# Expert weights in runs of 16 KB: packing the matrices so that one descriptor carries a partition's whole share

## The chip, the cores and the metric

The kernel runs on one core of one Trainium2 chip. The metric is device time in microseconds (us), the median of three runs of the kernel before: 660.63 us (658.98 to 662.78). The profile is of one more execution. Five engines matter: TensorE (PE, with its weight loads, PEld), VectorE (DVE), ScalarE (ACT), GpSimd (POOL) and SyncE (SP). SP, ACT and POOL also issue the transfers; all transfers of the core are carried out by the same 16 DMA engines. In the profile the queue of SP is q1, that of ACT q10 and that of POOL q0.

## What is computed

One layer of a hybrid decoder for 512 prompt tokens and 8 sample tokens, all float32: a mixer (an input projection, a gated recurrence on 512 channels and one on another 512, an output projection), then a hierarchical mixture of experts, then a final norm. Only the last part carries this change's weight:

```python
xn = rmsnorm(x, ln2_g)                       # 520 tokens x 1024
group = argmax(xn @ wg + bg)                 # 1 of 4 groups
top2  = two best of 8 experts in that group  # logits xn @ we[group] + be[group]
for each of 32 experts e, for its tokens:
    h = silu(xn @ w1[e]) * (xn @ w3[e])      # w1, w3: 1024 x 256
    y += gate * (h @ w2[e])                  # w2: 256 x 1024
out = rmsnorm(x + y, final_g)
```

Each of w1, w3 and w2 of an expert is 1 MB, so the 32 experts read 96 MB of weights from device memory, and every expert's weights are read whole, whatever the number of its tokens.

## The kernel before, in words

The mixer takes the first 310 us of the profile. Its input and output projections go by chunks of 2 MB (`w_in` in six chunks of 512 columns, `w_out` in two), which SP loads into the two halves of tile WC (L424).

Then the tokens are routed, and the experts are worked off in 16 pairs of two experts each (two experts side by side in TensorE's columns, up to 64 tokens each). Even pairs (called A below) use weight slots 0 and 1, odd pairs (B) slots 2 and 3. Slot 0 is in the tile SLOT0, slot 1 in SLOT1, slots 2 and 3 in WC and GY (w1 and w3) and in WC (w2). Expert 29 has a place of its own (XNT, XS).

For each pair n there are five pieces of work:

- the gather (POOL, L597): an indirect DMA that brings the 128 token rows of the pair (4 KB each) from `xn_rows` into T. A row without a token is skipped by its index, but leaves a 4-byte packet;
- the turn (PE, L1617): eight transposes of those rows, then DVE scales them into XRC;
- up (PE, L1629): 16 products with w1 and w3 of the two experts, each recorded as two instructions; ACT and DVE make h of it;
- down (PE, L1653): the products with w2; ACT (L824) and DVE (L1299) copy the result out;
- the scatter (POOL, L609): an indirect DMA that writes the rows to `expert_rows`.

TensorE's order is written out by hand: turn(n+1), up(n), down(n-1), transpose of h(n), then the same with n one higher. POOL's order is: gather(n+3), scatter(n), gather(n+4), scatter(n+1), and so on: gather(n+4) stands behind scatter(n), which waits for the copies behind down(n).

The weight loads wait for their slot: SP loads w1 and w3 of a slot (L439) when up with that slot has ended (semaphore h_written); ACT loads w2 (L392) when down has ended, before it copies the result. Four experts and expert 29 are loaded ahead, 27 in the loop. Each load is 128 partitions wide. For w1 and w3 the eight k of a partition lie one after the other in device memory, 8 KB, but in the slot the columns of w1 and w3 alternate by k:

```python
W13 = [s[:, 0:4096].rearrange("p (k f) -> p k f", k=KD) for s in (SLOT0, SLOT1, WCF, GYF)]      # L231
sp.dma_start(w13[:, :, half * FE:(half + 1) * FE],                                              # L439
             w[0, e].rearrange("(p k) f -> p k f", k=KD)).then_inc(s_w13[slot], 16)
```

so that a run without a break is 256 numbers, 1 KB, and a 1 MB load is 1024 packets. A w2 load has runs of 8 KB (128 packets), a chunk of `w_in` or `w_out` runs of 2 KB.

Of the kernel before, what the change touches and what calls it, by code (L numbers as in the profile page):

```python
# [25 lines left out]
P = 128  # L26
# [4 lines left out]
KD = D // P  # L31
# [6 lines left out]
NE = GROUPS * PER_GROUP  # L38
FE = 256
CAP = 64  # L40
# [3 lines left out]
KEPT = NE - 3  # L44
# [14 lines left out]
ORDER = [XR, FX, Q, V, GR, G]  # L59
# [35 lines left out]

def build(nc, x_prompt, x_sample, state_hgrn, state_rglru, state_conv, lower_bounds, ln1_g, w_in,
          hgrn_norm_g, conv_w, conv_b, lru_wx, lru_bx, lru_wa, lru_ba, lru_lambda, w_out, ln2_g,
          router_wg, router_bg, router_we, router_be, exp_w1, exp_w3, exp_w2, final_g,
          y_prompt, y_sample, hgrn_p, rglru_p, conv_p, hgrn_s, rglru_s, conv_s):

    xn_dram = nc.dram_tensor("xn_rows", (TOK, D), F32).ap()
# [9 lines left out]
    with ExitStack() as ctx:  # L111
# [10 lines left out]
        WC = sb("WC", [P, 2, KD, 512])  # L122
        SLOT0 = sb("SLOT0", [P, 6144])
# [5 lines left out]
        SLOT1 = sb("SLOT1", [P, 3 * NH * TOK])  # L129
# [94 lines left out]
        XGT = [XRC[:, 1024 * j:1024 * (j + 1)].rearrange("p (k t) -> p k t", k=KD) for j in range(2)]  # L224
# [3 lines left out]

        GYF = GY[:, :, :].rearrange("p m t -> p (m t)")
        WCF = WC[:, :, :, :].rearrange("p a k t -> p (a k t)")  # L230
        W13 = [s[:, 0:4096].rearrange("p (k f) -> p k f", k=KD) for s in (SLOT0, SLOT1, WCF, GYF)]  # L231
        W2 = [s.rearrange("p (j d) -> p j d", j=2)
              for s in (SLOT0[:, 4096:6144], SLOT1[:, 4096:6144], WCF[:, 4096:6144], WCF[:, 6144:8192])]

        XNF = XNT[:, :, :].rearrange("p k t -> p (k t)")
# [2 lines left out]
        OUT = [SLOT1[:, D * c:D * (c + 1)] for c in range(NT)]  # L238


        W13_KEPT = XNF[:, 0:4096].rearrange("p (k f) -> p k f", k=KD)
        W2_KEPT = XS[:, :, :]
        FGB = T[:, 0, 4:6, :].rearrange("p a t -> p (a t)")

# [1 line left out]
        PS = [ctx.enter_context(nc.psum_tensor(f"ps{b}", [P, 512], F32)) for b in range(8)]  # L246
# [5 lines left out]
        s_wc = [sem(f"wc_in{i}") for i in range(2)]  # L252
# [83 lines left out]
        s_w13 = [sem(f"w13_in{i}") for i in range(5)]  # L336
# [52 lines left out]
            return VEC[:, v + m:v + m + 1]  # L389

        def load_w2(eng, e, slot):
            eng.dma_start(W2[slot], exp_w2[0, e].rearrange("(p j) d -> p j d", j=2)).then_inc(s_w2[slot], 16)  # L392

        def weights_of(p, two, kept):

# [4 lines left out]
        def loads(slot, r, n):  # L400

            if slot == 4:
                return 1
            return r * (NPAIR // 2 - (slot == KEPT % 4)) + n
# [4 lines left out]
        @block.sync  # L409
        def _(sp):  # L410
            sp.dma_start(X[:, 0, :], x_rows(0)).then_inc(s_x[0], 16)
            for i in range(1, NT):
                sp.dma_start(X[0:ROWS[i], i, :], x_rows(i)).then_inc(s_x[i], 16)
            w_in_v = w_in[0].rearrange("(p k) n -> p k n", k=KD)
            w_out_v = w_out[0].rearrange("(m p) n -> p m n", p=P)
            sp.dma_start(G1[:], ln1_g[0].rearrange("(p k) -> p k", k=KD)).then_inc(s_gain[0], 16)

            rows = [(lower_bounds, LB, 8), (hgrn_norm_g, HGG, 4), (conv_w[0], CW, 16), (conv_b, CB, 4), (lru_bx, BX, 4),
                    (lru_ba, BA, 4), (lru_lambda, LAM, 4), (state_rglru[0], H0, NS * NH)]
            for j in range(8):  # L420
                if j >= 2:
                    sp.wait_ge(s_wc_free, j - 1)
                src = w_in_v[:, :, ORDER[j] * 512:(ORDER[j] + 1) * 512] if j < 6 else w_out_v[:, :, (j - 6) * 512:(j - 5) * 512]
                sp.dma_start(WC[:, j % 2, :, :], src).then_inc(s_wc[j % 2], 16)  # L424
                if j == 0:
                    for src, at, n in rows:
                        sp.dma_start(PROW[at:at + n, :], src.rearrange("a (m p) -> (a m) p", p=P)).then_inc(s_par, 16)
                    sp.dma_start(CROW[:], state_conv[0].rearrange("b w (m p) -> (b w m) p", p=P)).then_inc(s_par, 16)
                if j == 1:
                    sp.dma_start(G2[:], ln2_g[0].rearrange("(p k) -> p k", k=KD)).then_inc(s_gain[1], 16)  # L430
                    sp.dma_start(WGt[:], router_wg[0].rearrange("(p k) g -> p (k g)", k=KD)).then_inc(s_rt, 16)
                    sp.dma_start(WEt[:], router_we[0].rearrange("g (p k) e -> p g (k e)", k=KD)).then_inc(s_rt, 16)
                    sp.dma_start(RB[:, 0:GROUPS], router_bg[0:1, :].to_broadcast([P, GROUPS])).then_inc(s_rt, 16)
                    sp.dma_start(RB[:, GROUPS:], router_be.rearrange("a g e -> a (g e)").to_broadcast([P, NE])).then_inc(s_rt, 16)

            def load_w13(e, slot, w13=None):
                w13 = W13[slot] if w13 is None else w13
                for half, w in enumerate((exp_w1, exp_w3)):
                    sp.dma_start(w13[:, :, half * FE:(half + 1) * FE],  # L439
                                 w[0, e].rearrange("(p k) f -> p k f", k=KD)).then_inc(s_w13[slot], 16)  # L440


            sp.wait_ge(s_y, NH + 1)
            sp.wait_ge(s_hp, 16 * NH)
            for e in range(2):
                load_w13(e, e)
                load_w2(sp, e, e)


            for i, c in enumerate(TILE_ORDER):  # L450
                sp.wait_ge(s_xs, NT + i + 1)
                sp.dma_start(xn_dram[c * P:c * P + ROWS[c], :], XS[0:ROWS[c], i % 2, :]).then_inc(s_xn[i % 2], 16)
            sp.dma_start(FGB, final_g.rearrange("(a d) -> a d", a=1).partition_broadcast(P)).then_inc(s_fg, 16)

            sp.wait_ge(s_opr, 2 * NT)
            for e in range(2, 4):
                load_w13(e, e)
                load_w2(sp, e, e)
            await_read(sp, ("lg", NT - 1))
            for i in range(2):  # L460
                sp.wait_ge(s_xg[i], 16)
            load_w13(KEPT, 4, W13_KEPT)
            for i in range(2):
                sp.wait_ge(s_xn[i], 16 * ((NT + 1 - i) // 2))
            sp.dma_start(W2_KEPT, exp_w2[0, KEPT].rearrange("(p j) d -> p j d", j=2)).then_inc(s_w2[4], 16)

            sp.wait_ge(s_rnd, 1)
            rounds = sp.value_load(NRND[0:1, 0:1], min_val=1, max_val=MAX_ROUNDS)
            with sp.Fori(0, rounds) as r:
                with sp.If(r > 0):  # L470

                    sp.wait_ge(s_yw, r * NE)
                    for e in range(4):
                        load_w13(e, e)
                        load_w2(sp, e, e)
                with sp.Fori(0, NE // 4 - 2) as i:
                    for slot in range(4):
                        sp.wait_ge(s_hw, r * NE + i * 4 + slot + 1)
                        load_w13(i * 4 + slot + 4, slot)
                for slot in range(4):  # L480
                    if NE - 4 + slot != KEPT:
                        sp.wait_ge(s_hw, r * NE + NE - 8 + slot + 1)
                        load_w13(NE - 4 + slot, slot)


            sp.wait_ge(s_rdone, rounds + 1)
            ye_v = ye_dram.rearrange("(t k) d -> t k d", k=2)
            for c in range(NT):
                sp.dma_start(YE[c][0:ROWS[c]], ye_v[c * P:c * P + ROWS[c]]).then_inc(s_ye[c], 16)
            for c in range(NT):  # L490
                sp.wait_ge(s_fin[c], 1)
                sp.dma_start(y_rows(c), OUT[c][0:ROWS[c]]).then_inc(s_out, 16)
            sp.wait_ge(s_out, 16 * NT)
# [870 lines left out]
        def _(pe):  # L1364
# [255 lines left out]
            def up(n, p, r, use, kept=False):  # L1620

                pe.wait_ge(s_xgt, 2 * n + 3)
                weights = [weights_of(p, two, kept) for two in range(2)]
                for w13, _, slot in weights:
                    pe.wait_ge(s_w13[slot], 32 * loads(slot, r, use + 1))
                for k in range(KD):
                    for two in range(2):
                        at = two * CAP
                        ins = pe.matmul(PS[2 + p][at:at + CAP, :], XGT[p][:, k, at:at + CAP], weights[two][0][:, k, :],  # L1629
                                        start=(k == 0), stop=(k == KD - 1), tile_position=(0, at), skip_group_check=True)  # L1630
                        if k == KD - 1:
                            ins.then_inc(s_hw, 1)
# [69 lines left out]

_INS = ["x_prompt", "x_sample", "state_hgrn", "state_rglru", "state_conv", "lower_bounds", "ln1_g", "w_in",
        "hgrn_norm_g", "conv_w", "conv_b", "lru_wx", "lru_bx", "lru_wa", "lru_ba", "lru_lambda", "w_out", "ln2_g",
        "router_wg", "router_bg", "router_we", "router_be", "exp_w1", "exp_w3", "exp_w2", "final_g"]
_OUTS = [(1, SEQ, D), (NS, 1, D), (1, 1, NH, P, P), (1, 1, 512), (1, 1, 3, 512),
         (1, NS, NH, P, P), (1, NS, 512), (1, NS, 3, 512)]

# [17 lines left out]
```

## Time and profile before

| | |
|---|---|
| time, median of 3 runs (lowest, highest) | 660.63 us (658.98, 662.78) |
| profiled execution, first to last instruction | 656.5 us |
| PE busy | 510.5 us (78%), mean granted clock 0.88 |
| DVE, ACT, POOL busy | 230.2, 142.6, 79.2 us |
| bytes moved | 144.62 MB, 90494 packets, of which 72197 under 2 KB |
| q1 (SP) | 79608 packets, 100.57 MB |
| q10 (ACT) | 3888 packets, 28.31 MB |
| q0 (POOL) | 6976 packets, 15.44 MB |

The profile is read by stages. From 0 to 310 us TensorE is busy nearly throughout and the DMA engines a third of the time. From 310 to 351 us the tokens are routed and the first pairs start. From 351 to 605 us the DMA engines are busy throughout and TensorE stops and starts. From 605 us on the last pair is finished, the expert rows are read back, combined and written. A granted clock of 1.00 is 2.4 GHz, 0.50 is 1.2 GHz.

### The profile page before, as it was taken

To read this page: it belongs to the slowest core of one execution; us is meant where nothing else is said; L and a number is where in the kernel's file an instruction comes from. 1 tells how busy PE (TensorE), PEld (TensorE's weight loads), DVE (VectorE), ACT (ScalarE), POOL (GpSimd) and SP (SyncE) were. 2 spreads that over 40 slices of the span, in tenths; PEclk is the share of its full clock that TensorE was granted. 3 is DMA by queue.
4 is the path that set the end of the run, shared out by engine and by line. 5 is a ranking of instruction groups with operands and counts; after the bars stand their busy time and mean duration, and the time that the engine had idled before them with its cause. 6 is when DMAs were issued, how large, how long until landed. Compare 5 with 4: busy or idle time off the path is not lost. (4 is left out here: it accounts for less than half of the span.)

```text
span 656.5 us, 6560 instructions
## 1 busy us (share of the span) xinstructions
PE 510.5 (78%) x2320; PEld 296.6 (45%) x2320; DVE 230.2 (35%) x519; ACT 142.6 (22%) x267; POOL 79.2 (12%) x129
## 2 busy tenths in 40 slices
PE   3999999999999989999459839395684929478800
PEld 3788888358888733545333313132231313123200
DVE  3353112694987565233721111111020111101158
ACT  7211044704256352212100000000010000001123
POOL 4000000100211211000030111102011111101014
PEclk9899999999999979999559869788795969779955
DMA  9403110412341439210969999999999999969263
GB/s 300 151 0 129 57 72 12 152 53 77 100 165 64 144 122 308 116 44 22 342 230 331 375 376 337 388 336 394 336 369 376 355 379 331 398 198 381 82 280 130
DMA packets 90494, 144.62 MB, mean 220 GB/s; under 512 B 6489, under 2 KB 72197, under 8 KB 85856
## 3 DMA queue, kind: packets, MB, share of 16 engines
q1 hardware_dynamic: 79608, 100.57, 45.9%
q10 hardware_dynamic: 3888, 28.31, 10.6%
q0 software_dynamic: 6976, 15.44, 7.1%
q8 instruction: 14, 0.23, 0.2%
q14 instruction: 8, 0.07, 0.0%
HBM read 137.49 MB, written 15.10 MB: 232 GB/s over the span
## 5 line engine op out<-in xcount | busy, mean ns | idle before, releaser
L1390 PE MATMUL ps<-XNT,WC 128*128 128x260 f32 x640 | 144.8, 386 | 1.2 <-PE ps L1390 0.6
L1390 PEld LDWEIGHTS ps<-XNT,WC 128*128 128x128 f32 x640 | 121.9, 192 | 23.3 <-issue 4.0
L1629 PE MATMUL ps<-WC,XRC 128*64 128x512 f32 x128 | 69.0, 700 | 66.7 <-DMA GY<-in_exp_w 66.7
L1294 DVE TENSOR_TENSOR XRC<-ps,XRC 128x256 f32<-128x256 f32 x16 | 6.8, 424 | 184.2 <-ACT XRC L810 184.2
L1629 PE MATMUL ps<-GY,XRC 128*64 128x512 f32 x128 | 69.0, 701 | 0.0
L1629 PEld LDWEIGHTS ps<-WC,XRC 128*64 128x64 f32 x128 | 19.8, 162 | 107.7 <-issue 107.6
L1629 PE MATMUL ps<-SLOT,XRC 128*64 128x512 f32 x240 | 59.0, 617 | 2.4 <-DMA SLOT<-in_exp_w 2.4
L1551 PE MATMUL ps<-WC,GY 128*128 128x512 f32 x128 | 58.6, 611 | 1.0 <-DVE GY L1184 0.6
L810 ACT ACTIVATE XRC<-ps 128x256 f32<-128x256 f32 x16 | 6.1, 383 | 209.2 <-PE ps L1629 209.2
L609 POOL DMA_INDIRECT expert_rows<-T,SIDX x16 | 16.1, 1008 | 236.9 <-ACT T L824 220.1
L1551 PEld LDWEIGHTS ps<-WC,GY 128*128 128x128 f32 x128 | 24.4, 196 | 29.4 <-issue 28.2
L1629 PEld LDWEIGHTS ps<-SLOT,XRC 128*64 128x64 f32 x240 | 18.1, 142 | 37.4 <-issue 34.1
L1617 PE MATMUL ps<-IDENT,T 128*128 128x128 f32 x128 | 19.3, 299 | 14.0 <-DMA T<-xn_rows,GIDX 12.7
L1289 DVE TENSOR_TENSOR XRC<-ps,G 128x512 f32<-128x512 f32 x32 | 20.6, 685 | 25.8 <-PE ps L1617 25.8
L1653 PE MATMUL ps<-WC,XRC 128*64 128x512 f32 x128 | 28.9, 593 | 0.6 <-ACT XRC L814 0.6
L1653 PE MATMUL ps<-SLOT,XRC 128*64 128x512 f32 x120 | 28.9, 592 | 0.0
L1439 PE MATMUL ps<-WC,XNT 128*128 128x512 f32 x64 | 28.2, 596 | 0.3 <-DVE Vt L1022 0.3
L1299 DVE COPY T<-ps 128x512 f32<-128x512 f32 x16 | 11.1, 691 | 44.3 <-PE ps L1653 44.3
L1617 PEld LDWEIGHTS ps<-IDENT,T 128*128 128x128 f32 x128 | 16.8, 197 | 15.6 <-issue 13.7
L824 ACT ACTIVATE T<-ps 128x512 f32<-128x512 f32 x16 | 9.6, 597 | 64.7 <-issue 50.3
L1374 PE MATMUL ps<-IDENT,XS 128*128 128x128 f32 (+1 forms) x80 | 13.6, 320 | 10.4 <-ACT XS L669 10.3
L1629 PEld LDWEIGHTS ps<-GY,XRC 128*64 128x64 f32 x128 | 19.9, 163 | 0.0
(273 smaller groups left out, 587.7 us busy)
## 6 DMA issues: line engine op xcount, KB each, us to landing
SLOT<-in_exp_w SPq DMA_DIRECT2D x32, 1024.0 KB, 12.4
WC<-in_exp_w SPq DMA_DIRECT2D x18, 1024.0 KB, 13.3
GY<-in_exp_w SPq DMA_DIRECT2D x16, 1024.0 KB, 17.7
WC<-in_exp_w ACTq DMA_DIRECT2D x14, 1024.0 KB, 8.5
SLOT<-in_exp_w ACTq DMA_DIRECT2D x13, 1024.0 KB, 8.8
WC<-in_w_in SPq DMA_DIRECT2D x6, 2048.0 KB, 9.2
WC<-in_w_out SPq DMA_DIRECT2D x2, 2048.0 KB, 7.8
X<-in_x_prompt SPq DMA_DIRECT2D x4, 512.0 KB, 4.7
```

The source lines that it names most:

```text
L609: pool.indirect_dma_start(out=ye_dram, out_offset=bass.IndirectOffsetOnAxis(ap=SIDX[:, p, :].bitcast(U32), axis=0), in_=YO[p], in_offset=None,
L824: act.activation(YO[p][:, 0:512], PS[5][:, :], ACT.Copy).then_inc(s_ya, 1)
L1289: dve.tensor_tensor(XGT[p][:, 4 * j:4 * j + 4, :], PS[j][:, :].rearrange("p (k t) -> p k t", k=4), bc(G2[:, 4 * j:4 * j + 4], 2, P), ALU.m ...
L1294: dve.tensor_tensor(HG[p], PS[2 + p][:, FE:2 * FE], HS[p], ALU.mult).then_inc(s_hg, 1)
L1299: dve.tensor_copy(YO[p][:, 512:1024], PS[6][:, :]).then_inc(s_yd, 1)
L1374: ins = pe.transpose(ps[:, k * P:k * P + n], xv[:, 4 * j + k, :], IDENT[0:n, 0:n])
L1390: ins = pe.matmul(ps[:, 0:HALF], WC[:, j % 2, k, m * P:(m + 1) * P], XNT[:, k, hf * HALF:(hf + 1) * HALF], start=(k == 0), stop=(k == KD - 1))
L1439: ins = pe.matmul(ps[:, :], XNT[:, k, c * P:(c + 1) * P], WC[:, 1, k, :], start=(k == 0), stop=(k == KD - 1))
L1551: ins = pe.matmul(ps[:, :], rows, weights, start=(j == 0), stop=(j == 2 * NH - 1), skip_group_check=True)
L1617: ins = pe.transpose(PS[k // 4][:, (k % 4) * P:(k % 4 + 1) * P], xv[:, k, :], IDENT[:])
L1629: ins = pe.matmul(PS[2 + p][at:at + CAP, :], XGT[p][:, k, at:at + CAP], weights[two][0][:, k, :], start=(k == 0), stop=(k == KD - 1), tile ...
L1653: ins = pe.matmul(PS[5 + half][at:at + CAP, :], HT[p][:, j, at:at + CAP], weights[two][1][:, j, half * 512:(half + 1) * 512], start=(j == ...
```

## The change

Three arrays become one. `kernel()` lays w1, w3 and w2 of an expert side by side, by partition: `exp_w[e, p]` has 2048 numbers of w1, 2048 of w3 and 2048 of w2. The slot takes the same order (w1 whole, then w3 whole), so that one transfer of 16 KB runs brings what two transfers of 1 KB runs brought; the semaphore of a slot counts 16 for it and no longer 32. The w2 run stays 8 KB, with 24 KB instead of 8 KB between the starts of two runs in device memory. The up product reads its 512 moving columns as two pieces of 256. `w_in` and `w_out` are laid out chunk by chunk, with 16 KB runs. The same bytes are moved to the same tiles.

```diff
-        W13 = [s[:, 0:4096].rearrange("p (k f) -> p k f", k=KD) for s in (SLOT0, SLOT1, WCF, GYF)]
+        W13 = [s[:, 0:4096].rearrange("p (two k f) -> p two k f", two=2, k=KD) for s in (SLOT0, SLOT1, WCF, GYF)]
...
         def load_w2(eng, e, slot):
-            eng.dma_start(W2[slot], exp_w2[0, e].rearrange("(p j) d -> p j d", j=2)).then_inc(s_w2[slot], 16)
+            eng.dma_start(W2[slot], exp_w[e, :, 4096:].rearrange("p (j d) -> p j d", j=2)).then_inc(s_w2[slot], 16)
...
-                src = w_in_v[:, :, ORDER[j] * 512:(ORDER[j] + 1) * 512] if j < 6 else w_out_v[:, :, (j - 6) * 512:(j - 5) * 512]
-                sp.dma_start(WC[:, j % 2, :, :], src).then_inc(s_wc[j % 2], 16)
+                src = w_in[ORDER[j]] if j < 6 else w_out[j - 6]
+                sp.dma_start(WC[:, j % 2, :, :].rearrange("p k n -> p (k n)"), src).then_inc(s_wc[j % 2], 16)
...
             def load_w13(e, slot, w13=None):
                 w13 = W13[slot] if w13 is None else w13
-                for half, w in enumerate((exp_w1, exp_w3)):
-                    sp.dma_start(w13[:, :, half * FE:(half + 1) * FE],
-                                 w[0, e].rearrange("(p k) f -> p k f", k=KD)).then_inc(s_w13[slot], 16)
+                sp.dma_start(w13.rearrange("p two k f -> p (two k f)"), exp_w[e, :, 0:4096]).then_inc(s_w13[slot], 16)
...
                 for w13, _, slot in weights:
-                    pe.wait_ge(s_w13[slot], 32 * loads(slot, r, use + 1))
+                    pe.wait_ge(s_w13[slot], 16 * loads(slot, r, use + 1))
...
-                        ins = pe.matmul(PS[2 + p][at:at + CAP, :], XGT[p][:, k, at:at + CAP], weights[two][0][:, k, :],
+                        out = PS[2 + p][at:at + CAP, :].rearrange("t (two f) -> t two f", two=2)
+                        ins = pe.matmul(out, XGT[p][:, k, at:at + CAP], weights[two][0][:, :, k, :],
                                         start=(k == 0), stop=(k == KD - 1), tile_position=(0, at), skip_group_check=True)
...
+    inputs["exp_w"] = _np.concatenate([inputs.pop(name)[0].reshape(NE, P, -1) for name in ("exp_w1", "exp_w3", "exp_w2")], axis=2)
+    inputs["w_in"] = inputs["w_in"][0].reshape(P, KD, 6, 512).transpose(2, 0, 1, 3).reshape(6, P, KD * 512)
+    inputs["w_out"] = inputs["w_out"][0].reshape(KD, P, 2, 512).transpose(2, 1, 0, 3).reshape(2, P, KD * 512)
```

The order on PE, DVE, ACT and POOL stays as it was. On SP, in the loop over the experts, the load of a slot is two transfers behind one wait in the kernel before (SLOT0, SLOT1, WC and GY are slots 0 to 3; `in_exp_w1` and `in_exp_w3` are w1 and w3):

```order
L439 ISA [waits h_written]
L439 DMA SLOT0<-in_exp_w1 128x8x256
L439 DMA SLOT0<-in_exp_w3 128x8x256
L478 REGISTER_ALU
L439 ISA [waits h_written]
L439 DMA SLOT1<-in_exp_w1 128x8x256
L439 DMA SLOT1<-in_exp_w3 128x8x256
```

In the kernel after, the same place on SP reads:

```order
L436 ISA [waits h_written]
L436 DMA SLOT0<-in_exp_w 128x4096
L474 REGISTER_ALU
L436 ISA [waits h_written]
L436 DMA SLOT1<-in_exp_w 128x4096
```

Two transfers of 128x8x256 have become one of 128x4096 behind the same wait; nothing else has moved.

## Rows read from the trace of the kernel before

**Rows 1.** Stretches of the loop: bounds, length, engines' busy us (count), granted clock, DMA share, GB/s.

```profile
351.40:390.40 39.00, 25.37 (x117) 9.53 (x117) 6.09 (x10) 2.51 (x6) 4.93 (x8) 0.87 1.06 370
390.40:578.60 188.20, 128.84 (x580) 50.13 (x581) 24.04 (x40) 12.55 (x30) 24.49 (x40) 0.82 1.05 363
```

**Rows 2.** Waits of PE from 280 to 620 us: total, times, longest.

```profile
PE ps L1629 <- DMA GY<-in_exp_w: 66.7, 7, 11.5
PE ps L1617 <- DMA T<-xn_rows,GIDX: 12.7, 6, 6.1
```

**Rows 3.** Weight loads of w1 and w3 as SP issues them: start, us.

```profile
399.25 1.25 SPq L439 DMA_DIRECT2D WC<-in_exp_w  x2
...
411.15 18.88 SPq L439 DMA_DIRECT2D SLOT<-in_exp_w  x4
...
587.07 1.25 SPq L439 DMA_DIRECT2D WC<-in_exp_w  x2
```

**Rows 4.** Timeline of one cycle of two pairs: start, us, engine, line, what.

```profile
390.40 1.08 PE L1629 MATMUL ps<-WC,XRC 128*64 128x512 f32 x1 [11.25 <-DMA GY<-in_exp_w]
...
398.90 3.62 PE L1653 MATMUL ps<-SLOT,XRC 128*64 128x512 f32 x16
...
403.78 7.09 PE L1629 MATMUL ps<-SLOT,XRC 128*64 128x512 f32 x32
...
405.24 1.02 POOL L609 DMA_INDIRECT expert_rows<-T,SIDX  x1 [21.54 <-ACT T L824]
...
407.31 1.04 POOL L597 DMA_INDIRECT T<-xn_rows,GIDX  x1 [0.85 <-POOL GIDX L594]
...
414.51 0.86 ACTq L392 DMA_DIRECT2D WC<-in_exp_w  x2
...
415.55 1.16 PE L1617 MATMUL ps<-IDENT,T 128*128 128x128 f32 x8 [0.82 <-DMA T<-xn_rows,GIDX]
...
426.91 1.08 PE L1629 MATMUL ps<-WC,XRC 128*64 128x512 f32 x1 [10.21 <-DMA GY<-in_exp_w]
```

**Rows 5.** Transfers by queue, 430 to 434 us: packets, MB, share.

```profile
q1 hardware_dynamic: 1375, 1.39, 109.6%
```

**Rows 6.** Transfers, 630.5 to 638.5 us: the reading of expert rows.

```profile
DMA packets 462, 3.38 MB, mean 422 GB/s; under 512 B 50, under 2 KB 50, under 8 KB 50
```

**Rows 7.** Transfers by queue, 411.5 to 412.5 us.

```profile
q10 hardware_dynamic: 45, 0.37, 88.8%
q1 hardware_dynamic: 46, 0.05, 12.9%
q0 software_dynamic: 47, 0.00, 2.7%
```

**Rows 8.** Transfers by queue, 405.3 to 409.4 us, all queues that moved.

```profile
q1 hardware_dynamic: 730, 0.74, 56.4%
q10 hardware_dynamic: 106, 0.87, 52.5%
```

**Rows 9.** Transfers of q0, 409.4 to 414.9 us.

```profile
q0 software_dynamic: 288, 0.45, 21.8%
```

**Rows 10.** Page, queues of the whole execution, packets, MB, share: the instruction queue.

```profile
q8 instruction: 14, 0.23, 0.2%
```

**Rows 11.** PE in the first pair, 335 to 350 us.

```profile
335.92 1.97 PE L1617 MATMUL ps<-IDENT,T 128*128 128x128 f32 x8 [6.13 <-DMA T<-xn_rows,GIDX]
...
341.17 7.71 PE L1629 MATMUL ps<-SLOT,XRC 128*64 128x512 f32 x32
```

**Rows 12.** The last cycle: PE at the start of pair 15.

```profile
605.35 1.08 PE L1629 MATMUL ps<-WC,XRC 128*64 128x512 f32 x1 [2.64 <-DMA GY<-in_exp_w]
```

**Rows 13.** Waits of PE from 0 to 260 us: the longest but one.

```profile
PE ps L1504 <- DVE XS L1108: 2.0, 1, 2.0
```

**Rows 14.** Transfers by queue, 339.1 to 343.6 us, all queues that moved.

```profile
q1 hardware_dynamic: 1196, 1.21, 86.5%
```

**Rows 15.** POOL from 339 us: the third gather.

```profile
339.09 1.03 POOL L597 DMA_INDIRECT T<-xn_rows,GIDX  x1 [0.85 <-POOL GIDX L594]
```

More of the change, by code:

```diff
@@ L97, in build @@
           hgrn_norm_g, conv_w, conv_b, lru_wx, lru_bx, lru_wa, lru_ba, lru_lambda, w_out, ln2_g,
-          router_wg, router_bg, router_we, router_be, exp_w1, exp_w3, exp_w2, final_g,
+          router_wg, router_bg, router_we, router_be, exp_w, final_g,
           y_prompt, y_sample, hgrn_p, rglru_p, conv_p, hgrn_s, rglru_s, conv_s):
@@ L238, in build @@
         OUT = [SLOT1[:, D * c:D * (c + 1)] for c in range(NT)]
-        W13_KEPT = XNF[:, 0:4096].rearrange("p (k f) -> p k f", k=KD)
+        W13_KEPT = XNF[:, 0:4096].rearrange("p (two k f) -> p two k f", two=2, k=KD)
         W2_KEPT = XS[:, :, :]
@@ L413, in _ @@
                 sp.dma_start(X[0:ROWS[i], i, :], x_rows(i)).then_inc(s_x[i], 16)
-            w_in_v = w_in[0].rearrange("(p k) n -> p k n", k=KD)
-            w_out_v = w_out[0].rearrange("(m p) n -> p m n", p=P)
             sp.dma_start(G1[:], ln1_g[0].rearrange("(p k) -> p k", k=KD)).then_inc(s_gain[0], 16)
@@ L464, in _ @@
                 sp.wait_ge(s_xn[i], 16 * ((NT + 1 - i) // 2))
-            sp.dma_start(W2_KEPT, exp_w2[0, KEPT].rearrange("(p j) d -> p j d", j=2)).then_inc(s_w2[4], 16)
+            sp.dma_start(W2_KEPT, exp_w[KEPT, :, 4096:].rearrange("p (j d) -> p j d", j=2)).then_inc(s_w2[4], 16)
             sp.wait_ge(s_rnd, 1)
@@ L1704 @@
         "hgrn_norm_g", "conv_w", "conv_b", "lru_wx", "lru_bx", "lru_wa", "lru_ba", "lru_lambda", "w_out", "ln2_g",
-        "router_wg", "router_bg", "router_we", "router_be", "exp_w1", "exp_w3", "exp_w2", "final_g"]
+        "router_wg", "router_bg", "router_we", "router_be", "exp_w", "final_g"]
 _OUTS = [(1, SEQ, D), (NS, 1, D), (1, 1, NH, P, P), (1, 1, 512), (1, 1, 3, 512),
@@ L1713 @@
     from concourse.bass_utils import run_bass_kernel_spmd as _run
+    f32 = _np.float32
+    inputs = {name: _np.asarray(a, f32) for name, a in inputs.items()}
+    inputs["exp_w"] = _np.concatenate([inputs.pop(name)[0].reshape(NE, P, -1) for name in ("exp_w1", "exp_w3", "exp_w2")], axis=2)
+    inputs["w_in"] = inputs["w_in"][0].reshape(P, KD, 6, 512).transpose(2, 0, 1, 3).reshape(6, P, KD * 512)
+    inputs["w_out"] = inputs["w_out"][0].reshape(KD, P, 2, 512).transpose(2, 1, 0, 3).reshape(2, P, KD * 512)
     nc = _bacc.Bacc("TRN2", target_bir_lowering=False, num_devices=1)
```

## The prediction

> **What bounds the kernel now.** I read the table of stretches first, then the waits of TensorE, then one cycle of the expert loop in order of time, then the transfers by queue in short windows.
>
> The table of stretches [rows 1] gives the place: from 351.4 to 578.6 us the DMA engines are full (share 1.05 to 1.06) and move 363 to 370 GB/s, while TensorE is busy two thirds of the time. A cycle of two pairs (A with slots 0 and 1, B with slots 2 and 3) takes 188.2 / 5 = 37.64 us. The waits [rows 2] name what TensorE lacks: 66.7 us in 7 waits for the weights of B, but also 12.7 us for gathered rows. Both matter below.
>
> The cycle [rows 4] is lopsided. Up of B starts at 390.40, when its weights land. Down of A follows at 398.90 (3.62 us), up of the next A at 403.78 without a wait, the next turn at 415.55, and then TensorE stands until 426.91 for the weights of the next B. So weights end last there. But the second-last is close behind: the turn at 415.55 waited 0.82 us for a gather that was issued at 407.31, behind the scatter of 405.24, which itself waits for down of A. That chain (up of B, down of A, copies, scatter, gather, turn, next up of B) needs 416.7 - 390.40 = 26.3 us of the 37.64. Nothing may be gained below what this chain becomes after the change.
>
> **The rate of the runs.** A queue that moves 1 KB runs alone shows 1375 packets in 4 us on 16 engines [rows 5]: 0.0465 us each, 348 GB/s. Runs of 8 KB alone reach 422 GB/s [rows 6]: 0.311 us each. No load here has 16 KB runs. At the rate of the 8 KB runs one takes 0.621 us. The only 16 KB packets in the trace, of instructions, take about 0.002 x 656.5 x 16 / 14 = 1.5 us [rows 10]; that other end is for another kind of transfer beside full queues, so I stay with 0.621. Had 16 KB cost 16 times the 1 KB, it were 0.74. The pair's w1 and w3, 256 packets of 1 KB per engine, take 11.9 us of an engine now and 16 x 0.621 = 9.9 us then.
>
> The Trainium skill ("DMA: Bandwidth & Descriptors", section "Where 436 GB/s comes from") says that reading device memory binds at about 358 GB/s for a core. By that rule 348 could hardly rise and a 16 KB run would take 0.73 us. The trace disagrees for 8 KB runs, 422 GB/s [rows 6], and the measurement decides.
>
> **What the longer run does to the other queues.** In the window in which all three queues have work, each moves the same number of packets, 45, 46 and 47 in 1 us [rows 7], whether a packet is 8 KB, 1 KB or 4 bytes. So the engines take one packet of each queue in turn, and a round of the three costs 16 / 46 = 0.348 us, of which the 1 KB packet is 0.0465 and the other two 0.301. A scatter and the gather behind it are 288 packets of q0, 18 rounds of an engine, and they took from 409.4 to 414.9 us, 5.5 us [rows 9]. After the change a round is 0.621 + 0.301 = 0.92 us, plus 0.06 for the 110 of the 288 packets that are rows of 4 KB (0.45 MB; 0.155 us each at 422 GB/s): 0.98. Eighteen rounds are 17.7 us, 12.2 more.
>
> This holds if q1 and q10 are backlogged over the whole of those 17.7 us. They are: w1 and w3 of B are issued after up of B (399.25 [rows 3]) and need 16 rounds; at the first packet of q0 about 5 are left (an estimate: some 8 us of running time before it, at 0.62 us alone and 0.92 beside w2); those of the next A, issued at 411.15, bring 16 more. On q10 w2 of A has begun before 409.4 [rows 8] and w2 of B is issued at 414.51 [rows 4], 16 rounds each.
>
> **The sum, cycle by cycle.** The next turn would start 12.2 us later than 415.55, 37.35 us after up of B. TensorE has then stood long, and such a turn takes 1.97 us at half clock [rows 11] instead of 1.16. So the next up of B starts 39.4 us after the last. The weights are there earlier (5 rounds after the first packet of q0, 24 us after up of B), so the gather ends last. One credit: up right behind a slow turn takes 7.71 us [rows 11], where up after a long wait takes about 8.7 (390.40 to just before 399.25): the slow stretch is spent on the turn. That makes 38.4 us a cycle, +0.8 over 37.64, and for five cycles +3.8.
>
> The first cycle (351.4 to 390.4, 39.0 us [rows 1]) starts with a warm up of 7.1 us [rows 4] instead of 8.7, so its chain is 39.4 - 1.6 = 37.8: -1.2. The last one has no gather: pair 15 waits from the issue of its weights at 587.07 to 605.35 [rows 3, 12] for transfers alone, which become 2.0 us shorter, and up before it 1.0 shorter: -3.0. What follows 605.35 stays.
>
> Edits at nothing: the chunks of `w_in` and `w_out` (0.4 us sooner each by the rates above). TensorE's waits up to 260 us hold none for WC, so they are hidden behind its own products; the danger is that the runs of 16 KB hold up POOL's state loads in the same way, and TensorE's wait for those is 2.0 us [rows 13]; I take 0, bounds 0 to +2. One transfer instead of two on SP: SP's issue stretches of up to 18.88 us [rows 3] are waits for room in its queue, which nobody else waits for: 0, and without that cover at most the 2.0 us already counted. The up products read two pieces of 256 columns; nothing in the trace shows that form; same columns and bytes, so 0; if each of 16 records per operand pair cost 5% of 0.59 us, half a microsecond a pair, it would lie on the chain: 0 to +4 over the loop. The 24 KB spacing of w2: 0, since q10 is not late.
>
> Sum: -1.2 + 3.8 - 3.0 = -0.4 us on the span of 656.5, and the median of the runs is 4.1 above that span: 660.2. The transfers gain 5 us a cycle and the gather loses it again. Forecast 660 us, no change. The uncertain terms: 18 rounds at 0.93 to 1.03 are 0.9 us a cycle either way, the credit 1.0; six cycles make 650 to 674.
>
> **Rivals.**
>
> 1. The transfers stay the bound. If a run of 16 KB is served in pieces of 8 KB or less, a round stays at 0.67 us, 18 of them 12.1, and the chain is 32.8 us. A cycle moves 363 x 37.64 = 13.7 MB, at 422 GB/s 32.4 us, 5.2 less than now; over the 6.75 cycles from 351.4 to 605.35 that is 35 us: 626. The same if up of A and B came at even distances, since then q1 empties before the gather needs the engines. For it: full engines and 66.7 us of waits for weights [rows 1, 2]. Against it: packets of 8 KB are served whole, in turn with 4 bytes [rows 7], and the loop starts lopsided.
>
> 2. Slower: q0 starts later still. The first packet of q0 comes 4.2 us after the scatter's issue [rows 4, 8]. If that delay is a number of rounds that are already taken in, and not a time, it grows with the run. Five more rounds are 4.6 us, on the chain in each of six cycles: 28 us, 688. Against it: with 1 KB runs of q1 alone, rounds of under 0.1 us, the gather of 339.09 shows no packet before 343.6, the same 4.5 us [rows 14, 15]. It decides from 0.6 us a cycle, which makes the kernel slower by 0.5%.
>
> 3. The rate cap of the skill's rule. With 0.73 us for 16 KB a round is 1.09, 18 of them 19.6: +1.9 a cycle, 672. Against it stands the 422 GB/s.
>
> **Chances.** Forecast 0.58; rival 1 0.32, rival 2 0.08, rival 3 0.02. Half a per cent, 3.3 us, is about what a measurement can tell here (the three runs spread by 0.3% either way). Within the forecast's 650 to 674 I give 0.16 to faster, 0.22 to no change and 0.20 to slower, since its terms of unknown size lean up. With the rivals: faster 0.48, same 0.22, slower 0.30. The range reaches to most of rival 1 and leaves out rival 2: 622 to 680. The likeliest case's own is 650 to 674.
>
> **What would show it.** Right: TensorE's wait for weights in up is nearly gone, its wait for gathered rows in the turn has grown from 12.7 to some 70 to 95 us (13 us in each of six cycles, and the first gather); the gathers for A land 18 to 21 us after their issue; q1, q10 and q0 move equal counts in the window of the scatter; the DMA engines idle about 6 us of a cycle; SP issues each load at once. Wrong: gathers that land within 12 us, or up still waiting for weights with the engines at 410 GB/s or more (rival 1), or a first packet of q0 later than 5 us after the scatter's issue (rival 2), or up of B over 9 us.

## The result and the profile after

The changed kernel takes 651.16 us in the median of 4 runs (650.40 to 655.36), the kernel before 660.65 us beside it (658.98 to 662.78). The ratio is 0.9869, with an interval of 0.9832 to 0.9907: 9.5 us or 1.3% faster. The span of the profiled execution fell from 656.5 to 648.9 us, 7.6 us; the profiled execution of before was one of the quicker ones, which is the rest of the difference. Where an experiment below gives 639.74 us as its highest time, that one execution ran at a lower granted clock than the others of its kernel (0.873 against 0.901 to 0.915), and the ratio leaves it out.

The waits of TensorE from 270 to 620 us answer to [rows 2]; the columns are the total, the number and the longest:

```profile
PE ps L1613 <- DMA T<-xn_rows,GIDX: 71.2, 7, 12.3
PE ps L1602 <- DVEq L1268: 4.0, 1, 4.0
```

The 66.7 us of waiting for weights are gone altogether. In their place stand 71.2 us of waiting for gathered rows, 12.7 before. TensorE waits for something else for nearly as long.

The stretches by the starts of up of B answer to [rows 1], with the same columns and the last step added:

```profile
352.70:389.60 36.90, 24.59 (x117) 9.80 (x116) 4.80 (x8) 2.51 (x6) 4.93 (x8) 0.86 0.99 410
389.60:575.80 186.20, 132.72 (x583) 51.10 (x583) 24.03 (x40) 12.55 (x30) 24.48 (x40) 0.82 0.88 365
575.80:599.10 23.30, 23.30 (x109) 8.31 (x109) 4.42 (x8) 1.64 (x4) 1.21 (x2) 0.97 0.66 266
```

Five cycles take 186.2 us, 37.24 each, where they took 37.64. The DMA share fell from 1.05 to 0.88: the difference of the two shares is some 6 us of a cycle in which the engines now idle, and the bytes still arrive at 365 GB/s. The transfers no longer set the length of a cycle.

One cycle in order of time, which answers to [rows 4]:

```profile
387.74 1.97 PE L1613 MATMUL ps<-IDENT,T 128*128 128x128 f32 x8 [12.31 <-DMA T<-xn_rows,GIDX]
...
389.64 1.12 PE L1626 MATMUL ps<-WC,XRC 128*64 128x512 f32 x1
...
398.12 3.60 PE L1650 MATMUL ps<-SLOT,XRC 128*64 128x512 f32 x16
...
398.49 0.33 SPq L436 DMA_DIRECT2D WC<-in_exp_w  x1
...
404.48 1.02 POOL L605 DMA_INDIRECT expert_rows<-T,SIDX  x1 [23.59 <-ACT T L820]
406.55 1.04 POOL L593 DMA_INDIRECT T<-xn_rows,GIDX  x1 [0.85 <-POOL GIDX L590]
...
410.25 0.93 SPq L436 DMA_DIRECT2D SLOT<-in_exp_w  x2
...
424.20 1.97 PE L1613 MATMUL ps<-IDENT,T 128*128 128x128 f32 x8 [10.26 <-DMA T<-xn_rows,GIDX]
```

From turn to turn it is 36.46 us: 1.90 to up of B, 14.84 to the scatter (as before: 390.40 to 405.24), then 19.72 us until the rows that were ordered behind that scatter are there. Before, the last piece was 10.3 us. SP issues both loads of the next A within 0.93 us, where it stood for 18.88 us [rows 3].

Why the rows take longer shows in the transfers by queue (packets, MB, share). First 404.5 to 408.2 us, behind the scatter's issue, as [rows 8]:

```profile
q1 hardware_dynamic: 91, 1.23, 77.7%
q10 hardware_dynamic: 48, 0.39, 25.1%
```

No packet of q0 has come yet. Then 408.5 to 412.5 us, a stretch like [rows 7], now 4 us long:

```profile
q1 hardware_dynamic: 62, 1.02, 59.3%
q10 hardware_dynamic: 60, 0.49, 29.0%
q0 software_dynamic: 60, 0.25, 14.9%
```

The queues move 62, 60 and 60 packets: one each in turn, as before. A round now takes about 4 x 16 / 61 = 1.05 us, against 0.348; the packets of q0 are rows of 4 KB here and were 4 bytes in [rows 7]. Last, 408.5 to 423.2 us, in which the 288 packets of the scatter and the gather are served, as in [rows 9]:

```profile
DMA packets 837, 6.26 MB, mean 426 GB/s; under 512 B 242, under 2 KB 242, under 8 KB 353
...
q1 hardware_dynamic: 257, 3.69, 58.7%
q10 hardware_dynamic: 291, 2.12, 34.2%
q0 software_dynamic: 289, 0.46, 8.2%
```

The first of the 288 packets starts at 408.69 and the last ends at 423.00: 14.3 us. In the kernel before they ran from 409.62 to 414.80, 5.2 us; the 5.5 of [rows 9] is the window around them.

### The profile page after: what moved, and what is told of

Read it like the earlier page. It is cut to its first block and busy times, and to the rows that moved or that the text cites. A ratio compares the mean times of both kernels' runs of the same rounds, so it can differ in the third digit from the quotient of the medians.

```text
span 648.9 us, 6503 instructions
## 1 busy us (share of the span) xinstructions
PE 510.7 (79%) x2320; PEld 297.1 (46%) x2320; DVE 230.2 (35%) x519; ACT 142.7 (22%) x267; POOL 79.2 (12%) x129
## 3 DMA queue, kind: packets, MB, share of 16 engines
q1 hardware_dynamic: 10488, 100.57, 39.3%
## 5 line engine op out<-in xcount | busy, mean ns | idle before, releaser
L1613 PE MATMUL ps<-IDENT,T 128*128 128x128 f32 x128 | 24.3, 352 | 72.6 <-DMA T<-xn_rows,GIDX 71.2
L1626 PE MATMUL ps<-GY,XRC 128*64 128x512 f32 x128 | 66.8, 682 | 0.0
L1626 PE MATMUL ps<-WC,XRC 128*64 128x512 f32 x128 | 66.8, 682 | 0.0
L1547 PE MATMUL ps<-WC,GY 128*128 128x512 f32 x128 | 57.1, 598 | 2.6 <-DVE GY L1180 2.1
L1613 PEld LDWEIGHTS ps<-IDENT,T 128*128 128x128 f32 x128 | 20.4, 208 | 74.3 <-issue 72.4
L1626 PEld LDWEIGHTS ps<-WC,XRC 128*64 128x64 f32 x128 | 19.3, 158 | 41.7 <-issue 41.4
L1650 PE MATMUL ps<-WC,XRC 128*64 128x512 f32 x128 | 28.9, 593 | 0.6 <-ACT XRC L810 0.6
L1370 PE MATMUL ps<-IDENT,XS 128*128 128x128 f32 (+1 forms) x80 | 14.3, 332 | 11.1 <-ACT XS L665 10.7
L1626 PEld LDWEIGHTS ps<-GY,XRC 128*64 128x64 f32 x128 | 19.3, 158 | 0.0
```

Of the source, the lines that this page charges most:

```text
L1370: ins = pe.transpose(ps[:, k * P:k * P + n], xv[:, 4 * j + k, :], IDENT[0:n, 0:n])
L1547: ins = pe.matmul(ps[:, :], rows, weights, start=(j == 0), stop=(j == 2 * NH - 1), skip_group_check=True)
L1613: ins = pe.transpose(PS[k // 4][:, (k % 4) * P:(k % 4 + 1) * P], xv[:, k, :], IDENT[:])
L1626: ins = pe.matmul(out, XGT[p][:, k, at:at + CAP], weights[two][0][:, :, k, :], start=(k == 0), stop=(k == KD - 1), tile_position=(0, at), ...
L1650: ins = pe.matmul(PS[5 + half][at:at + CAP, :], HT[p][:, j, at:at + CAP], weights[two][1][:, j, half * 512:(half + 1) * 512], start=(j == ...
```

## The experiments

The question was first whether the gather behind full rounds is really what eats the gain, and second how much each part of it weighs. Every ratio below is against the kernel before, run on the same chip (medians 661.72 us for the first four, 660.58 us for the last three).

**Loads of 8 KB runs, the rest as changed.** This keeps the packed array and halves the packet:

```diff
-    sp.dma_start(w13..., exp_w[e, :, 0:4096]).then_inc(s_w13[slot], 16)
+    for half in range(2):
+        sp.dma_start(w13[:, half]..., exp_w[e, :, 2048 * half:2048 * (half + 1)]).then_inc(s_w13[slot], 16)
-    pe.wait_ge(s_w13[slot], 16 * loads(slot, r, use + 1))
+    pe.wait_ge(s_w13[slot], 32 * loads(slot, r, use + 1))
```

> The changed kernel, but w1 and w3 of an expert come as two transfers of 8 KB runs (same packed arrays). Theory (after the change the chain scatter, gather, turn ends last, because q0 has 18 packets per engine to pass and each waits for one q1 and one q10 packet): a round falls from 0.611 + 0.309 + 0.06 = 0.98 us to 0.68, 18 rounds by 5.4 us, so the cycle of two pairs falls from 37.4 to about 32.4 us, where the transfers (13.7 MB at about 425 GB/s) end last again: about 620 to 628 us, TensorE's wait for gathered rows well under 71 us, its wait for weights back. Rival (the gather is late for a reason that has nothing to do with the length of q1's packets, such as its place in GpSimd's order alone, or full DMA engines): 651, within 3 us, gathers wait 71 us as before.

Measured: 627.07 us (625.61 to 639.74), ratio 0.9463 (0.9432 to 0.9493). TensorE's longest waits from 270 to 620 us:

```profile
PE ps L1615 <- DMA T<-xn_rows,GIDX: 45.5, 7, 7.5
...
PE ps L1628 <- DMA GY<-in_exp_w: 2.1, 2, 1.7
```

And the stretch of three cycles, from turn to turn (engines' busy us, clock, DMA share, GB/s):

```profile
383.20:481.70 98.50, 78.16 (x349) 30.32 (x349) 14.43 (x24) 7.54 (x18) 14.69 (x24) 0.86 1.01 417
```

A cycle is 98.5 / 3 = 32.8 us, the engines are full again, and a gather of the loop lands 13.2 us after its issue in the median (16.8 in the changed kernel, 8.2 before). So some 24 us hang on the length of the packets, with the same bytes in the same place; the only other difference is two loads for each expert instead of one. The rival fell. One part of the expectation did not come out: the wait for weights did not come back, it is 2.1 us in all. Gather and transfers now end almost together: the wait is still named after the gather, yet the DMA share is 1.01.

**The gather issued one scatter earlier, 16 KB kept.** Gather(n+4) goes ahead of scatter(n) instead of behind it:

```diff
+    gather(base + 3, slice(3, 4), 1)
     with pool.Fori(0, NPAIR // 2 - 2) as i:
...
-            gather(base + q + 3, bass.ds(q + 3, 1), 1 - p)
+            gather(base + q + 4, bass.ds(q + 4, 1), p)
             scatter(base + q, bass.ds(q, 1), p, r * (NPAIR // 2) + i)
-    gather(base + NPAIR - 1, slice(NPAIR - 1, NPAIR), 1)
```

> The changed kernel with GpSimd's order altered: gather(n+4) is issued before scatter(n) instead of behind it, so it no longer waits for down of pair n and its 9 packets per engine no longer stand behind the 9 of the scatter. Theory: TensorE's wait for gathered rows in the turn (71 us) all but goes, the transfers end last, a cycle of about 32.4 us, 618 to 628 us. Rival (the engines are simply full, and a gather issued earlier takes its time from the weights, so the wait moves to up): above 640.

Measured: 624.06 us (621.23 to 625.00), ratio 0.9421 (0.9386 to 0.9456), the fastest kernel of this study. TensorE's waits from 270 to 620 us:

```profile
PE ps L1626 <- DMA GY<-in_exp_w: 23.6, 7, 5.0
PE ps L1626 <- DMA SLOT<-in_exp_w: 13.7, 6, 4.1
PE ps L1613 <- DMA T<-xn_rows,GIDX: 5.4, 1, 5.4
```

And three cycles, from up of B to up of B:

```profile
379.50:476.60 97.10, 77.86 (x348) 31.15 (x348) 14.42 (x24) 7.54 (x18) 15.94 (x27) 0.92 1.01 425
```

The gathers land later than ever, 24.3 us after their issue in the median and 28.1 at most, and after the first one nobody waits for them. What is left are waits for weights of a few us, for A and for B alike, at 425 GB/s and 32.4 us a cycle. So the late rows were the whole of the bound in the changed kernel, and what lies under them is the transfers at full rate.

**The same move in the kernel before**, to see whether the earlier gather is worth anything by itself (the edit is the one above).

> The kernel before (1 KB runs) with the same alteration of GpSimd's order as in e2. Theory: in the kernel before the weights end last by 10 us a cycle, so an earlier gather gains nothing: 657 to 662 us; TensorE's wait for gathered rows falls from 12.7 to about 6 us (the first gather), that for weights grows by as much. Rival (the gather chain held the kernel before as well): under 650.

Measured: 660.59 us, ratio 0.9990 (0.9969 to 1.0011). Its waits:

```profile
PE ps L1629 <- DMA GY<-in_exp_w: 73.8, 7, 12.7
PE ps L1617 <- DMA T<-xn_rows,GIDX: 5.6, 1, 5.6
```

The wait for rows went and the wait for weights took it over, 66.7 to 73.8 us. With 1 KB runs the earlier gather gives nothing, with 16 KB runs it gives 27 us. The packing gives 9.5 us alone and some 37 together with the earlier gather.

**Only the chunks of `w_in` and `w_out` packed**, the experts as before:

```diff
-    src = w_in_v[:, :, ORDER[j] * 512:...] if j < 6 else w_out_v[...]
-    sp.dma_start(WC[:, j % 2, :, :], src).then_inc(s_wc[j % 2], 16)
+    src = w_in[ORDER[j]] if j < 6 else w_out[j - 6]
+    sp.dma_start(WC[:, j % 2, :, :].rearrange("p k n -> p (k n)"), src).then_inc(s_wc[j % 2], 16)
```

> The kernel before with only w_in and w_out packed by chunk (16 KB runs instead of 2 KB); experts as before. Theory: TensorE waits for no chunk before 260 us, so nothing changes: 659 to 662 us. Rival (part of the 9.5 us gained by the whole change comes from the mixer): 655 or less.

Measured: 661.43 us, ratio 0.9998 (0.9981 to 1.0014). This part of the change is worth nothing either way, to 0.2%.

**Both: earlier gather and 8 KB runs** (the two edits together).

> Both alterations: gather(n+4) before scatter(n), and w1 and w3 as two transfers of 8 KB runs. Theory: once the gather is early the transfers end last, and 8 KB runs move nearly as fast as 16 KB runs (0.309 us against half of 0.611), so the two gains do not add: 620 to 627 us, as e2 (624). Rival (the rounds still cost time elsewhere, in the scatters or in w2): another 10 us less than e2, 615 or below.

Measured: 625.96 us (625.50 to 626.65), ratio 0.9488 (0.9464 to 0.9512). The gains don't add, as each leads to the same bound: the waits are for weights again, and beside 8 KB runs alone (0.9463) the earlier gather shows no gain. The rival, 615 or below, fell.

```profile
PE ps L1628 <- DMA GY<-in_exp_w: 39.7, 7, 8.4
PE ps L1615 <- DMA T<-xn_rows,GIDX: 5.5, 1, 5.5
```

**Loads of 4 KB runs, in the order of the changed kernel**, four transfers for each expert:

```diff
+    flat = w13.rearrange("p two k f -> p (two k f)")
+    for at in range(0, 4096, 1024):
+        sp.dma_start(flat[:, at:at + 1024], exp_w[e, :, at:at + 1024]).then_inc(s_w13[slot], 16)
```

> The changed kernel in its own order, but w1 and w3 of an expert come as four transfers of 4 KB runs. Theory: a round falls to 0.16 + 0.31 + 0.06 = 0.53 us, 18 rounds to at most 9.5, the gather chain to some 30 us a cycle, so that the transfers end last: 13.7 MB at a mean of about 415 GB/s (4 KB runs take 0.160 us, 410 GB/s) are 33 us a cycle: 622 to 630 us; TensorE's wait for gathered rows under 30 us. Rival (fewer and longer packets are better throughout): above 640.

Measured: 632.58 us (630.30 to 633.91), ratio 0.9577 (0.9543 to 0.9611): 5.5 us behind 8 KB, and above the range I expected.

```profile
PE ps L1628 <- DMA GY<-in_exp_w: 30.9, 7, 9.0
PE ps L1615 <- DMA T<-xn_rows,GIDX: 17.5, 6, 5.5
PE ps L1628 <- DMA SLOT<-in_exp_w: 6.2, 4, 3.5
```

The rows now come soon (10.4 us after the issue at most), and the cycle waits mostly for the weights of B, as in the kernel before. Five cycles of this kernel, then five of the one with 8 KB runs, from up of B to up of B:

```profile
385.26:556.68 171.42, 131.28 (x580) 51.44 (x581) 24.04 (x40) 12.56 (x30) 24.48 (x40) 0.87 1.02 407
385.14:551.88 166.74, 130.85 (x581) 51.05 (x580) 24.04 (x40) 12.56 (x30) 24.50 (x40) 0.87 1.01 414
```

The engines are full in both, and 34.3 us a cycle at 407 GB/s stand against 33.3 at 414, so most of the 5.5 us goes with the lower rate; what else lowers it beside the shorter run was not taken apart. Over the packet length the time thus has its lowest tried point in the middle: 1 KB 660.65, 4 KB 632.58, 8 KB 627.07, 16 KB 651.16. The 1 KB point is the kernel before; it also differs in its chunks, which the run above showed to be worth nothing, and in the form of up's operand and the layout in device memory, which were not run alone.

**16 KB on q1, but w2 on q10 in 4 KB runs.** The round is made shorter at the other queue; each w2 load becomes two transfers:

```diff
-    eng.dma_start(W2[slot], exp_w[e, :, 4096:]...).then_inc(s_w2[slot], 16)
+    for j in range(2):
+        at = 4096 + D * j
+        eng.dma_start(W2[slot][:, j, :], exp_w[e, :, at:at + D]).then_inc(s_w2[slot], 16)
```

> The changed kernel with 16 KB runs for w1 and w3, but w2 as two transfers of 4 KB runs. Theory (a packet of q0 waits for one packet of each of the other queues, so q10's length counts as q1's does): a round falls from 0.98 to 0.61 + 0.16 + 0.06 = 0.83 us, 18 rounds by at most 2.7 us, less some 0.7 us that ScalarE needs for two more issues before its copy: 1 to 2 us a cycle, six cycles, 639 to 646 us. Rival (only q1 counts): 651 or, with the issues, 655.

Measured: 632.94 us (632.18 to 635.57), ratio 0.9602 (0.9568 to 0.9635). The rival by which only q1 counts fell, but the time lies below the range I expected: the gain is 6 us more than the most that I had worked out. Two turns in the order of time:

```profile
386.02 1.97 PE L1616 MATMUL ps<-IDENT,T 128*128 128x128 f32 x8 [10.30 <-DMA T<-xn_rows,GIDX]
...
419.55 1.97 PE L1616 MATMUL ps<-IDENT,T 128*128 128x128 f32 x8 [8.12 <-DMA T<-xn_rows,GIDX]
```

And the transfers by queue in 4 us of the same cycle, 410 to 414:

```profile
q1 hardware_dynamic: 60, 0.95, 55.4%
q10 hardware_dynamic: 172, 0.63, 38.7%
q0 software_dynamic: 178, 0.20, 14.0%
```

From turn to turn it is 33.5 us. In the 4 us shown, q10 and q0 again move equal counts, 172 and 178, but q1 only 60. I had priced full rounds of three. The thin rounds come between two loads: the last 16 KB packet for B starts at 409.5, the first for the next A at 411.2. From 409.4 to 411.0:

```profile
q10 hardware_dynamic: 127, 0.46, 70.1%
q0 software_dynamic: 121, 0.17, 28.9%
q1 hardware_dynamic: 15, 0.02, 2.9%
```

With the shorter rounds B's weights are through sooner, and q0 moves 121 packets while q1 has next to nothing. Over five cycles this gap of q1 lasts 1.3 to 2.0 us, in the changed kernel 0.6 to 1.1. The 288 packets of scatter and gather take 10.9 to 11.8 us in six cycles, 3.4 less in the mean than in the changed kernel, where I had priced at most 2.7.

## Why the prediction came out as it did

The forecast was 660 us, no change; the kernel is 1.3% faster and inside the range. The mechanism was right at nearly every step and the balance of its two sides was not. That the time fell inside the range says little: 622 to 680 took in most of the first rival too, and 651 is at the lower edge of the 650 to 674 of the likeliest case. The positions of up of B along the span (before, after) say where the 7.6 us came from: 351.37 and 352.69 for the first, then 390.40 and 389.64, 578.6 and 575.7, 605.35 and 599.13. So +1.3 came ahead of the first, -2.1 in the first cycle, -2.1 in the next five, -3.4 in the last, and a further -1.7 in the last up; some 0.3 us were given back behind it. The sum had -1.2, +3.8 and -3.0 for the three middle ones and nothing for the other three.

**What bounds it next: right.** The wait for weights vanished, the wait for rows grew to 71.2 us (70 to 95 said), and the gathers for A landed 17.4 to 19.3 us after their issue (18 to 21 said). The second-last release named from [rows 4] was the one that came out.

**The rate of a 16 KB run: right.** In 402 to 405 us q1 runs alone:

```profile
DMA packets 78, 1.26 MB, mean 421 GB/s; under 512 B 1, under 2 KB 1, under 8 KB 1
```

That is 3 x 16 / 77 = 0.62 us a packet on an engine. The third rival falls with it, as the trace of before had already told. The Trainium skill ("DMA: Bandwidth & Descriptors", "Where 436 GB/s comes from") says that the side of device memory binds such transfers at about 358 GB/s; the 421 GB/s measured here, with the kernel on one core, disagree, and the same section also names 425 GB/s as measured for 16 MB.

**One packet of each queue in turn: right**, 62, 60 and 60.

**The 18 rounds at 17.7 us: the step that failed.** They took 14.3 in the cycle shown, and 13.9 to 16.2, 14.8 in the mean, over all six cycles (5.2 to 6.3 and 5.6 before). The step said that q1 and q10 are backlogged with long packets over the whole of it. The window of 408.5 to 423.2 shows what was there: q1 moved 3.69 MB, 225 packets of 16 KB or 14.1 an engine, q10 259 of 8 KB or 16.2 an engine, in 18 rounds. The other packets of q1 and q10, 32 and 32, are 2 an engine of 4 bytes, one behind each load that ends in the window, and they take a turn of their own: only with them does q10 come to 291 packets beside 289 of q0. In two more rounds q1 had nothing. Part of both lies between the loads of B and those of A, 412.5 to 414 us, where q0 moves two packets for one of q1:

```profile
q10 hardware_dynamic: 65, 0.40, 63.7%
q1 hardware_dynamic: 31, 0.25, 38.8%
q0 software_dynamic: 64, 0.02, 4.9%
```

Priced by the prediction's own packet times, 3.9 x 0.62 + 1.8 x 0.31 = 3.0 us less: 14.7. The same count holds in the other cycles. Over the six, q1 had 12.1 to 16.3 long packets an engine and q10 15.7 to 16.6, and with the packet times of this trace (0.611, 0.309 and 0.159 us for 16, 8 and 4 KB) the sum of what was moved comes within 0.4 us of the measured time in each.

**The credit of 1.0 us a cycle: failed**, the other way. Up behind the slow turn was to take 7.7 us to the end of its last product. It took 8.66 (389.64 to 398.29), like the 8.68 behind a long wait before; over the five cycles the means are 8.98 and 8.96. The clock in four pieces from the turn on (the column behind the engines):

```profile
387.70:389.70 2.00, 1.96 (x10) 1.64 (x11) 0.00 (x0) 0.00 (x0) 0.00 (x0) 0.50 1.03 438
389.70:391.50 1.80, 1.80 (x7) 0.57 (x8) 1.29 (x2) 0.00 (x0) 0.00 (x0) 0.50 1.00 421
391.50:393.00 1.50, 1.50 (x8) 0.40 (x6) 0.00 (x0) 0.00 (x0) 0.00 (x0) 0.55 1.02 426
393.00:398.50 5.50, 5.50 (x28) 1.80 (x26) 0.00 (x0) 0.13 (x1) 0.00 (x0) 1.00 0.43 174
```

After the 12.31 us of standing, the clock is granted at half (1.2 GHz) through the turn and through 3.3 us or so of up, though TensorE was already working in the turn. The single row on which the credit rested [rows 11] was no rule: the first up behind a slow turn takes 8.93 us in the changed kernel, where nothing on TensorE had changed but the form of the operand:

```profile
341.29 8.93 PE L1626 MATMUL ps<-SLOT,XRC 128*64 128x512 f32 x32
```

That is also the +1.3 us ahead of the first cycle. The form of the operand does not explain it by itself, as the ranges overlap: this first up takes 7.97 and 8.31 us in the two runs above that keep the old form, and 8.06 to 8.93 in those with the new one. Why the clock rises earlier in one execution than in another stays open.

With both terms put right the cycle of the sum is 38.4 - 3.4 + 1.0 = 36.0 us, and 36.46 was measured in the cycle shown; the difference is mostly the time from the gather's last packet to the turn, 1.2 us (423.0 to 424.20) instead of 0.65. (The sum's 39.4 should read 39.3, 37.35 + 1.97.) The cycle shown is one of the short ones. In the five cycles from 389.64 to 575.74, 37.2 us each, the means are 15.2 us from up of B to the scatter's issue, 4.2 to the first packet, 14.5 for the 288 packets, 1.4 to the turn and 1.9 to up. So the packets took 3.2 us less than the sum had, and the way from up to the scatter (1.3, the credit in it) and the end of the gather (0.8) took most of that back.

**The last cycle: right in size**, -3.0 forecast and -3.4 measured, with some luck. The forecast left pair 15 waiting for transfers that are 2.0 us shorter. In fact TensorE is busy for all of the 23.30 us of the stretch and pair 15 waits for nothing: the 2.64 us of [rows 12] are gone, and up ahead of it, the only one in the loop that took the credit, is 0.7 us shorter (7.77 for 8.45). A further gain was left out. The last up, with no wait ahead of it, now starts at full clock (2.4 GHz):

```profile
599.13 0.61 PE L1626 MATMUL ps<-WC,XRC 128*64 128x512 f32 x1
...
605.62 0.59 PE L1626 MATMUL ps<-GY,XRC 128*64 128x512 f32 x1
```

From its first to its last product 6.5 us, where before it was 8.1 (605.35 to 613.49): another 1.7 us.

**The edits at nothing: right for the chunks** (0.9998). The operand read in two pieces shows no cost: a product takes 592 ns in the median in both kernels. SP's issue became short, from up to 18.88 us to at most 0.93, and nothing more came of it; with 8 KB runs, again two transfers for a slot, four of them issue in 1.98 us, so it hangs on the number of packets and not of transfers. The wider spacing of w2 shows no cost: a packet of q10 takes 0.342 x 14.7 x 16 / 259 = 0.31 us, as [rows 6].

**The rivals.** The first, transfers stay the bound at 626 us, did not come out in this kernel, and it had the right price for what lies beneath: 624.06 us with 32.4 us a cycle once the rows are out of the way. The second, a later start of q0, fell: the first q0 packet comes 4.2 us after the scatter's issue (404.48 to 408.69), with rounds three times as long. Before it was 4.4 (405.24 to 409.62); the prediction's 4.2 reaches to the edge of its window.

## What to carry to other kernels

Where queues are served packet by packet in turn, a longer run speeds up its own queue and lengthens the round of every other one; before making runs longer, look for a queue with many small packets on the path, and count its packets times the new round. Here it turned a gain of 37 us into one of 9.5, and either a run of middle length or an earlier order of the small transfers got it back. When an edit moves little, try it together with the one that frees the next-latest release: an edit worth nothing alone may be worth most of it.

## What the runs showed of the hardware that was not expected

- The 4-byte packet behind each load takes a whole turn of its queue among the others: 32 on q1 and 32 on q10 in the 14.7 us of one scatter and gather, and with its 32 q10 moves 291 packets beside 289 of q0.
- The start of a scatter did not depend on the length of the packets ahead of it: 4.2 us after the issue with 16 KB, 4.4 us with 1 KB on q1. With no other queue at work it is 1.55 us, as for the last two scatters (611.46 to 613.00).
- Slow rows cost nothing by themselves: gathers that landed 24.3 us after their issue belonged to the fastest kernel (624.06 us).
- The half clock behind a long stand lasted through the turn and on into up. Behind such a turn up took 7.77 to 9.20 us in the changed kernel, behind a stand without one 8.45 to 9.20 before, so the turn ahead of it shortened it in one cycle of six.
